# Moving the gate row to the weighing of expert blocks, and a combine that sums on TensorE and normalises from PSUM

## The reference

```python
u = h * (1.0 + sc2[:, None, :]) + sh2[:, None, :]
ff = hier_moe(u, ...)          # top-1 group of 4, then top-2 of its 8 experts
h = layer_norm(DEEPNORM_ALPHA * h + gt2[:, None, :] * ff, ln2_g[l], ln2_b[l])

# inside hier_moe, for a block of slots with tokens tok_idx and expert e:
xb = h_pad[tok_idx]
hid = jax.nn.silu(xb @ w_gate[e]) * (xb @ w_up[e])
yb = hid @ w_down[e]
y = jnp.zeros((T + 1, D)).at[slot_tok].add(yb * slot_w[:, None])
```

## Time and profile before

| what | value |
|---|---|
| median of three runs | 2038.07 us (2036.42 to 2038.44) |
| profiled execution, its own time | 2041.03 us |
| its span | 2039.2 us |
| TensorE, VectorE, ScalarE busy | 90%, 71%, 52% of the span |
| mean granted clock | 0.954 of full speed |
| experts' loop, from the first transposes to the last product in the loop | 1344.5 to 1958.7 us |
| drain | 1958.7 to 1987.0 us |
| combine and last store | 1987.0 to 2039.2 us |

### The profile page before, as it was taken

How to read it: one execution, slowest core, us unless ns; L and a number is a source line. 1 busy time by engine, 2 the same in 40 slices (tenths; PEclk the granted TensorE clock), 3 DMA queues, 4 the chain that set the end, 5 groups by cost and what they waited for, 6 DMA issues and landing times. The chain is left out here.

```text
span 2039.2 us, 35190 instructions
## 1 busy us (share of the span) xinstructions
PE 1838.8 (90%) x14112; PEld 1041.8 (51%) x14112; DVE 1445.9 (71%) x1816; ACT 1053.4 (52%) x1271; POOL 356.1 (17%) x229
## 2 busy tenths in 40 slices
PE   4988869989978999998999999469999999999965
PEld 1555554434437999884444445334444444444432
DVE  5545555685766666645666768779999888888948
ACT  1455552345432333423342511149888888888944
POOL 0000000011101212110000000013444444444410
PEclk9999989999988999998999999679999999999988
DMA  8500007463255231105331312359999999999935
GB/s 313 100 22 22 1 1 278 166 235 137 105 186 122 65 79 50 48 2 166 85 99 57 114 62 83 134 210 410 402 404 411 406 395 401 396 392 388 386 131 211
DMA packets 164743, 391.33 MB, mean 192 GB/s; under 512 B 25324, under 2 KB 102757, under 8 KB 136960
## 3 DMA queue, kind: packets, MB, share of 16 engines
q1 hardware_dynamic: 149632, 357.87, 48.4%
q0 software_dynamic: 14976, 31.56, 4.1%
HBM read 361.68 MB, written 48.68 MB: 201 GB/s over the span
## 5 line engine op out<-in xcount | busy, mean ns | idle before, releaser
L2209 PE MATMUL ps<-w_gate_up_split,gathered_t 128*128 128x512 f16 x1728 | 387.7, 381 | 8.0 <-ACT gathered_t L2283 3.8
L2375 DVE SCALAR_TENSOR_TENSOR w_gate_up_split<-w_staged,w_gate_up_split 128x2048 f16<-128x2048 f32 x144 | 327.5, 2288 | 56.1 <-ACT w_gate_up_split L2274 55.0
L2274 ACT ACTIVATE w_gate_up_split<-w_staged 128x2048 f16<-128x2048 f32 x144 | 274.2, 1908 | 66.6 <-PEq L144 31.4
L2209 PEld LDWEIGHTS ps<-w_gate_up_split,gathered_t 128*128 128x128 f16 x1728 | 167.3, 98 | 208.7 <-ACT gathered_t L2283 10.2
L217 PE MATMUL ps<-u_transposed,w_gates_split 128*128 128x512 f16 x1152 | 253.7, 382 | 4.9 <-PEq L144 3.0
L813 PE MATMUL ps<-u_transposed,w_dense_split 128*128 128x512 f16 x1152 | 254.0, 383 | 4.3 <-DVE w_dense_split L188 3.5
L2236 PE MATMUL ps<-w_down_split,hidden_t 128*128 128x512 f16 x864 | 193.9, 381 | 7.7 <-ACT hidden_t L2320 4.5
L813 PEld LDWEIGHTS ps<-u_transposed,w_dense_split 128*128 128x128 f16 x1152 | 112.9, 99 | 147.4 <-issue 11.7
L217 PEld LDWEIGHTS ps<-u_transposed,w_gates_split 128*128 128x128 f16 x1152 | 113.1, 98 | 145.3 <-issue 12.7
L2375 DVE SCALAR_TENSOR_TENSOR w_down_split<-w_staged,w_down_split 128x2048 f16<-128x2048 f32 x72 | 164.1, 2286 | 20.7 <-ACT w_down_split L2274 20.5
L2274 ACT ACTIVATE w_down_split<-w_staged 128x2048 f16<-128x2048 f32 x72 | 137.0, 1907 | 45.9 <-DMA w_staged<-in_w_down 29.6
(11 more groups left out here) (358 smaller groups left out, 2956.6 us busy)
## 6 DMA issues: line engine op xcount, KB each, us to landing
w_staged<-in_w_gate SPq DMA_DIRECT2D x72, 1024.0 KB, 12.1
w_staged<-in_w_up SPq DMA_DIRECT2D x72, 1024.0 KB, 11.7
w_staged<-in_w_down SPq DMA_DIRECT2D x72, 1024.0 KB
w_dense_ring<-in_w_in SPq DMA_DIRECT2D x17, 1024.0 KB, 6.8
w_ada_ring<-in_w_ada SPq DMA_DIRECT2D x8, 2048.0 KB
w_gates_ring<-in_w_in SPq DMA_DIRECT2D x24, 512.0 KB, 6.5
qkv_scratch<-qkv_silu POOLq DMA_DIRECT2D x20, 512.0 KB, 3.6
w_ada_early<-in_w_ada SPq DMA_DIRECT2D x4, 2048.0 KB, 20.7
```

The lines of the kernel that those rows point to most:

```text
L2209: last = pe.matmul(ps[:, GU[s] + j, :], xt[:, s, xp, k, :], w16[:, j, wp, k, :], start=(k == 0 and t == 0), stop=(k == KC - 1 and t == 2))
L2274: nc.scalar.activation(split(kind, 0, int(q)), staged(m, kind, int(q)), ACT.Identity, scale=W_SCALE).then_inc(hi_ok[kind + q], 1)
L2375: nc.vector.scalar_tensor_tensor(split(kind, 1, int(q)), staged(m, kind, int(q)), W_SCALE, split(kind, 0, int(q)), ALU.mult, ALU.subtract) ...
```

## The change

`weigh` goes from ScalarE to VectorE and multiplies by the slot's weight and by the gate row at once. `copy_x` becomes one copy of both banks on ScalarE. In the combine TensorE adds three terms, the residual and both choices (six float32 matmuls a chunk). The sum stays in PSUM. ScalarE copies it to get the row sum (`total`), then takes squares about the mean (`variance`); VectorE makes the result in two passes (`normalise`), the first from PSUM.

```diff
             def product(j, i, s):
                 if j == 0:
-                    pe.wait_ge(S("x_hi"), n + 1)
-                    pe.wait_ge(S("x_lo"), n + 1)
+                    pe.wait_ge(S("x_copied"), n + 1)
...
-                    for k in range(2):
-                        last = pe.matmul(ps[...], m.ident[:], ys[:, c % RING, k, half * 512:half * 512 + 512],
-                                         start=(k == 0), stop=(k == 1))
+                    cols = slice(half * 512, half * 512 + 512)
+                    for k, term in enumerate((m.z1[:, c, cols], ys[:, c % RING, 0, cols], ys[:, c % RING, 1, cols])):
+                        last = pe.matmul(ps[...], m.ident[:], term, start=(k == 0), stop=(k == 2))
...
         @block.scalar
-                nc.scalar.activation(xt[:, s, 0]..., half16(0), ACT.Identity).then_inc(S("x_hi"), 1)
+                nc.scalar.activation(xt[:, s]..., ps[:, 0:2, :]....bitcast(F16), ACT.Identity).then_inc(S("x_copied"), 1)
-            def weigh(i, s):
-                act.wait_ge(used["down1"], n + 1)
-                if exists(i, s, 2):
-                    act.wait_ge(y_stored[s], i * 16)
-                nc.scalar.activation(y[:, s, :]..., ps[:, 6:8, :], ACT.Identity, scale=m.slot_weight[:, bass.ds(n, 1)]
-                                     ).then_inc(S("y_ready"), 1)
...
+            def total(c):
+                act.wait_ge(added, c + 1)
+                nc.scalar.activation(square[:, c % 2, :]..., ps[:, 2 * (c % 4):2 * (c % 4) + 2, :], ACT.Identity,
+                                     accum_out=tot[:, 0, c:c + 1]).then_inc(total_ok, 1)
+            def variance(c):
                 act.wait_ge(mean_ok, c + 1)
-                nc.scalar.activation(square[:, c % 2, :], m.z1[:, c, :], ACT.Square, bias=mean[:, c:c + 1], accum_out=tot[:, 1, c:c + 1])
+                nc.scalar.activation(square[:, c % 2, :]..., ps[...], ACT.Square, bias=mean[:, c:c + 1], accum_out=tot[:, 1, c:c + 1])
                 act.wait_ge(act_p, c + 1)
                 nc.scalar.activation(std[:, c:c + 1], tot[:, 1, c:c + 1], ACT.Sqrt, scale=1.0 / D, bias=eps[:, 0:1])
-            def unit(c):
-                act.wait_ge(shift_ok, c + 1)
...
-                nc.scalar.activation(res[:, c % 3, :], m.z1[:, c, :], ACT.Identity, scale=rstd[:, c:c + 1], bias=shift[:, c:c + 1])
+            total(0)
+            for c in range(TC):
+                variance(c)
+                if c < TC - 1:
+                    total(c + 1)
...
         @block.vector
-                nc.vector.tensor_copy(xt[:, s, 1]..., half16(1)).then_inc(S("x_lo"), 1)
+            def weigh(i, s):
+                dve.wait_ge(used["down1"], n + 1)
+                if exists(i, s, 2):
+                    dve.wait_ge(y_stored[s], i * 16)
+                nc.vector.scalar_tensor_tensor(y[:, s, :]..., ps[:, 6:8, :], m.slot_weight[:, bass.ds(n, 1)],
+                                               rows[:, 2, :]..., ALU.mult, ALU.mult).then_inc(S("y_ready"), 1)
             def work(i):
                 for s in range(2):
+                    weigh(*back(i, s, 3))
                     split_low("down", *back(i, s, 2))
-                    if exists(i, s, 1):
-                        split_low("gate", i, s)
-                        split_low("up", i, s, "0")
-                        hidden(*back(i, s, 1))
-                        copy_x(i, s)
...
+                    split_low("gate", i, s)
+                    split_low("up", i, s, "0")
+                    hidden(*back(i, s, 1))
                     split_low("up", i, s, "1")
                     hidden_low(*back(i, s, 1))
             turns(dve, work)
+            weigh(j, 1)
             split_low("down", j + 1, 0)
             hidden(j + 1, 1)
             hidden_low(j + 1, 1)
+            weigh(j + 1, 0)
             split_low("down", j + 1, 1)
+            weigh(j + 1, 1)
-            def sums(c):
...
-            def scalars(c):
...
-            def scale(c):
...
+            def minus_mean(c):
+                dve.wait_ge(total_ok, c + 1)
+                nc.vector.tensor_scalar(mean[:, c:c + 1], tot[:, 0, c:c + 1], -1.0 / D, None, ALU.mult).then_inc(mean_ok, 1)
+            def normalise(c):
+                dve.wait_ge(std_ok, c + 1)
+                step(nc.vector.reciprocal(rstd[:, c:c + 1], std[:, c:c + 1]))
+                if c >= 3:
+                    dve.wait_ge(out_done[c % 3], 16 * (c // 3))
+                result = res[:, c % 3, :]
+                nc.vector.scalar_tensor_tensor(result..., ps[...], mean[:, c:c + 1], rows[:, 0, :]..., ALU.add, ALU.mult).then_inc(sum_used, 1)
+                step.settle()
+                dve.wait_ge(sum_used, c + 1)
+                if c < TC - 1:
+                    minus_mean(c + 1)
+                nc.vector.scalar_tensor_tensor(result, result, rstd[:, c:c + 1], rows[:, 1, :], ALU.mult, ALU.add).then_inc(res_ok, 1)
+            minus_mean(0)
+            for c in range(TC):
+                normalise(c)
```

More of the change, by code:

```diff
@@ L2258, in _ @@
                 for half in range(2):
-                    for k in range(2):
-                        last = pe.matmul(ps[:, 2 * (c % 4) + half, :], m.ident[:], ys[:, c % RING, k, half * 512:half * 512 + 512],
-                                         start=(k == 0), stop=(k == 1))
+                    cols = slice(half * 512, half * 512 + 512)
+                    for k, term in enumerate((m.z1[:, c, cols], ys[:, c % RING, 0, cols], ys[:, c % RING, 1, cols])):
+                        last = pe.matmul(ps[:, 2 * (c % 4) + half, :], m.ident[:], term, start=(k == 0), stop=(k == 2))
                 last.then_inc(added, 1)
@@ L2324, in work @@
                     split_high("down", *back(i, s, 2))
-                    weigh(*back(i, s, 3))
                     split_high("gate", i, s)
@@ L2339, in _ @@
             split_high("down", j + 1, 0)
-            weigh(j, 1)
             silu(j + 1, 1)
@@ L2376, in split_low @@
                                                    ALU.mult, ALU.subtract).then_inc(lo_ok[kind + q], 1)
-            def copy_x(i, s):
+            def weigh(i, s):
                 if not exists(i, s):
@@ L2422, in _ @@
             hidden_low(j + 1, 1)
+            weigh(j + 1, 0)
             split_low("down", j + 1, 1)
+            weigh(j + 1, 1)
             step = Steps(dve, dve_p)
-            step(nc.vector.memset(eps[:], LN_EPS))
-            step.settle()
-            def sums(c):
-                zc, yc = m.z1[:, c, :], gated[:, c % 2, :]
-                dve.wait_ge(added, c + 1)
-                nc.vector.tensor_tensor(yc.rearrange("p (h n) -> p h n", h=2), ps[:, 2 * (c % 4):2 * (c % 4) + 2, :],
-                                        rows[:, 2, :].rearrange("p (h n) -> p h n", h=2), ALU.mult).then_inc(sum_used, 1)
-                dve.wait_ge(sum_used, c + 1)
-                step(nc.vector.scalar_tensor_tensor(zc, yc, 1.0, zc, ALU.mult, ALU.add, accum_out=tot[:, 0, c:c + 1]))
-                step.settle()
+            nc.vector.memset(eps[:], LN_EPS).then_inc(eps_ok, 1)
@@ L2445, in scale @@
-            def scale(c):
-                dve.wait_ge(unit_ok, c + 1)
-                step(nc.vector.tensor_tensor(res[:, c % 3, :], res[:, c % 3, :], rows[:, 0, :], ALU.mult))
-                step.settle()
-                nc.vector.tensor_tensor(res[:, c % 3, :], res[:, c % 3, :], rows[:, 1, :], ALU.add).then_inc(res_ok, 1)
-            for c in range(TC + 1):
-                if c < TC:
-                    sums(c)
-                if c >= 1:
-                    scalars(c - 1)
-                if c >= 2:
-                    scale(c - 2)
@@ L2458, in _ @@
-            scale(TC - 1)
+                if c >= 3:
+                    dve.wait_ge(out_done[c % 3], 16 * (c // 3))
+                result = res[:, c % 3, :]
+                nc.vector.scalar_tensor_tensor(result.rearrange("p (h n) -> p h n", h=2), ps[:, 2 * (c % 4):2 * (c % 4) + 2, :], mean[:, c:c + 1],
+                                               rows[:, 0, :].rearrange("p (h n) -> p h n", h=2), ALU.add, ALU.mult).then_inc(sum_used, 1)
+                step.settle()
+                dve.wait_ge(sum_used, c + 1)
```

45 lines of the change are left out of this document (12 added, 33 removed).

## The result

| | median, us | runs | profiled execution | its span |
|---|---|---|---|---|
| before, in the same comparison | 2039.55 (2036.21 to 2044.02) | 16 | 2041.03 | 2039.2 |
| after | 2046.51 (2041.11 to 2053.15) | 16 | 2048.09 | 2046.0 |

The account below looks back on a forecast made before the run. TensorE, then loads, then TensorE bound the loop; the drain is serial; VectorE bounds the combine, TensorE after the change. 0.7 - 0.4 + 0.12 - 0.06 = +0.36 us on 2038.07 gave 2038.4 us, range 2033.5 to 2043.5.

Parts of the forecast that it names:

- The loop, +0.7: Experts' loop: the longer copy delays TensorE once, in the last step paced by loads, by 0.7 us (bounds 0 and 0.9).
- Cost in this stretch: 0: Loop, where loads set the pace: the moved weighing costs 0 us, as four or more loads stand in line.
- The rival's 8.5 us: Loop, loads' stretch: VectorE becomes late and transfers get gaps, 0.5 us a block in 17 blocks, +8.5 us; chance 0.07.
- The drain, -0.4 + 0.12: Drain: the last down product starts 0.4 us earlier (bounds -1.0 and +0.2); the last weighing takes 0.12 us longer on VectorE.
- With the 0.7 from above: Drain: its start is moved by the loop's 0.7 us, so VectorE's weighing runs from 1967.6 to 1968.8.
- The weigh-first reckoning: Drain: VectorE weighs, then makes the first down half's low part by 1971.05; TensorE's last down product starts at about 1971.1.
- The combine, -0.06: Combine: TensorE becomes the bound at 5.13 us a chunk, then a serial tail of 5.77 us; end 2036.05 against 2036.11.
- the bound of +0.5: Combine: upper bound of its term, set by the bounds of the serial tail, 5.4 and 6.3 us.
- the transfers: Rival, loop: earlier stores and reloads bring 17.5 us a block back to 16.88, up to 10 us faster, 2028; chance 0.05.
- the clock in the combine: Rival, combine: TensorE's clock stays at its lower level throughout, +39 us, 2077; chance 0.01.
- the third term: Rival, combine: TensorE takes under about 0.53 us a product, so the added term is cheap; -14 us, 2024; chance 0.02.
- The 0.01 for something unseen on the slow side: Whole kernel: chance of 0.01 left for an unnamed cause of a slower result.

Follow-up runs that it names:

- split_copy: The changed kernel with the copy of the transposed rows on both engines, as before the change; ratio 1.0024 to the kernel before, loop 615.65 us.
- combine_part: The kernel before with the changed combine, the multiplication by the gate row left out; ratio 1.0008 to the kernel before, loop 615.22 us.
- loop_part: The changed kernel with the combine of before, so the gate row is applied twice; ratio 1.0029 to the kernel before, combine 52.96 us.
- early_residual: The changed kernel with the first three chunks' residual products issued while TensorE waits for the rows; ratio 1.0005 to the kernel before, combine 47.26 us.

## Why the prediction was wrong

**What bounds the kernel: right.** TensorE, loads, TensorE, then a serial drain and a combine with TensorE in VectorE's place. The loads' ring is still 17.5 us.

**The loop, +0.7: the copy right, the loads missed.** Copy (1.86) and weighing (1.28) cost what was reckoned, and the longer copy costs 0.64 us once, as reckoned. The term measured +1.3 to +2.9 in three profiles, mean +2.1, outside the bounds of 0 to 0.9. The step that failed is "Cost in this stretch: 0", with the copy of the last paced step still at its old start: it started 0.7 to 2.3 us later, waiting for its load, and split_copy, which has no longer copy, shows the same (1.5). The rival's 8.5 us did not come either. Through which buffer the weighing acts is not shown; combine_part, with the loop of before, has 1.1 us of such lag, so a part is not the edit's at all. The early cost of the copy was not 0 either (block 0's gate product waited 3.64 us for 3.04), but it was mostly swallowed later, as the forecast said.

**The drain, -0.4 + 0.12: the step that decided.** "With the 0.7 from above" moved block 34's down product by the loop's lag alone, and so took the exit as a constant. The weigh-first reckoning was right (3.88 us from product to product for 3.98), but the product ahead of it came 1.6 us later and took 2.7 longer. The term measured +3.9 on average over three profiles (28.41 to 32.29). The forecast left out the 2.80 us of "issue" at the exit and asked neither what the branch waits for nor what an earlier store would fall upon. It did say that rows would be stored some 2 us sooner, but looked at this only as a gain for the transfers. The first store of the drain was issued 4.4 to 4.7 us ahead of the branch instead of 0.2 to 0.4. That this store lengthens the branch fits all profiles and is not proven, and why the clock falls behind it is open.

**The combine, -0.06: nearly right.** The pace is 5.14 us a chunk ((2036.74 - 2000.75) / 7, total to total; 5.13 forecast). TensorE took 0.4 us and the tail 0.4 us more than reckoned, the tail's share for the hand-over between the passes. +0.7 on average over three profiles, just past the bound of +0.5, and loop_part's old combine shows the same +0.7.

**Rivals.** Neither the transfers nor the clock in the combine decided it, and the third term wasn't cheap (early_residual's six took 5.31 us at the full clock, 0.885 each with the first weight load). No rival held the case that came: the longer gap at the exit and the lower clock after it. The 0.01 for something unseen on the slow side was too little; a stage of 28 us without any overlap has no cover for a surprise.

## What to carry to other kernels

Work that is moved between engines changes when stores and loads are issued, and at a program's seams (the exit from a loop, a dependent tail) there is no cover: look at each "issue" gap on the path and at what would newly fall into it. Before a sum is moved to another engine, price it on both: the third term moved the bound from VectorE to TensorE at the same 5.1 us a chunk, where dropping one pass of VectorE alone took 7.7 us off the combine. And judge a 0.2% effect by medians of many runs: a single profile's stage sum was off from them by up to 3.1 us here.

## What the hardware did that was not expected

Leaving a loop is not free for TensorE. The branch took 4.0 to 6.5 us of its sequencer, 1.5 to 4.5 of them as idle time, with a 16 KB read of code in it that shares the DMA engines with 300 to 400 GB/s of loads. After such a gap the granted clock sometimes fell to the lower level for some 3 to 7 us (24 matmuls took 5.34, 7.03 or 8.06 us), and not in order of the gap's length. Ahead of the combine, products put into the wait ran at the full clock (5.31 us for six), but after a further wait of 4.1 to 4.5 us the next ones started at the lower one.
